# An eleventh weight slot, loaded between the two halves of the output projection's weights, and expert pairs written out

## The reference

```
mixed = sigmoid(gate_a) * (y_a @ moba_up) + sigmoid(gate_b) * (y_b @ hgrn_up)
x = x + mixed @ w_out
h2 = rmsnorm(x, norm2_w)
logits = h2 @ router_w + router_b            # top 4 of 32, softmax over the 4
gu = xg @ w_gate_up[e] + b_gate_up[e]        # 1024 -> 2048, for the tokens of expert e
y  = ((up + 1) * glu(gate)) @ w_down[e] + b_down[e]
out = rmsnorm(x + sum of w * y, final_norm_w)
```

## Time and profile before

| | us |
|---|---|
| median of three runs (1144.83 to 1147.44) | 1146.56 |
| the profiled execution's own time | 1146.84 |
| its span, first to last instruction | 1145.0 |
| TensorE busy | 1065.1 |
| VectorE busy | 349.5 |
| ScalarE busy | 222.9 |

### The profile page before, as it was taken

How to read it: one execution, slowest core, us unless ns; L and a number is a source line. 1 busy time by engine, 2 the same in 40 slices (tenths; PEclk the granted TensorE clock), 3 DMA queues, 4 the chain that set the end, 5 groups by cost and what they waited for, 6 DMA issues and landing times.

```text
span 1145.0 us, 13775 instructions
## 1 busy us (share of the span) xinstructions
PE 1065.1 (93%) x5611; PEld 521.7 (46%) x5611; DVE 349.5 (31%) x686; ACT 222.9 (19%) x354; POOL 37.5 (3%) x32
## 2 busy tenths in 40 slices
PE   7999999999999999998999898988888898999896
PEld 7789999734343443433333333333333333343332
DVE  4983788421213122121212111121212030213022
ACT  6734675301010101010101010100010101010002
POOL 0380000000000000000000000000000000000000
PEclk9999999999999999999999999999999998999999
DMA  9445658999999999999999999999999999999994
GB/s 324 163 159 185 265 187 291 367 369 430 428 428 428 430 428 427 428 428 430 425 428 429 428 428 426 430 428 429 430 425 430 428 429 425 428 430 428 428 428 191
DMA packets 46916, 439.28 MB, mean 384 GB/s; under 512 B 5324, under 2 KB 7656, under 8 KB 22152
## 3 DMA queue, kind: packets, MB, share of 16 engines
q1 hardware_dynamic: 44560, 436.78, 91.7%
q10 hardware_dynamic: 2296, 1.61, 0.5%
HBM read 437.32 MB, written 1.05 MB: 383 GB/s over the span
## 4 chain that ended last, share of the span: by engine, by line
PE 59%; DMA 36%; DVE 2%; issue 1%; SPq 1%; ACT 1%; DVEq 0%
PE PS L1652 23%; DMA S<-in_w_gate_up_dram 19%; PE PS L1702 11%; DMA EXTRA<-in_w_down_dram 8%; PE PS L1323 6%; DMA EXTRA<-in_w_gate_up_dram 4%; PE PS L1634 4%; DMA S<-in_w_down_dram 4%; PE PS L1614 3%; DMA S<-in_w_in_dram 1%; PE PS L1336 1%; PE PS L1339 1%; PE PS L1342 1%; PE PS L1689 1%; PE PS L1671 1%
## 5 line engine op out<-in xcount | busy, mean ns | idle before, releaser
L1652 PE MATMUL PS<-S,M 128*64 128x512 f32 x1664 | 378.7, 604 | 32.5 <-DMA S<-in_w_gate_up_dram 23.9
L1652 PEld LDWEIGHTS PS<-S,M 128*64 128x64 f32 x1664 | 115.9, 138 | 270.7 <-issue 222.7
L1702 PE MATMUL PS<-S,M 128*64 128x512 f32 x800 | 178.2, 595 | 18.2 <-DMA S<-in_w_down_dram 17.3
L1156 DVE TENSOR_SCALAR M<-PS 128x256 f32<-128x256 f32 x64 | 27.0, 422 | 537.2 <-PE PS L1652 537.2
L751 ACT ACTIVATE M<-M 128x256 f32<-128x256 f32 x64 | 26.7, 416 | 501.0 <-DVE M L1156 501.0
L1702 PEld LDWEIGHTS PS<-S,M 128*64 128x64 f32 x800 | 56.6, 137 | 129.0 <-issue 109.5
L756 ACT COPY M<-PS 64x512 f32<-64x512 f32 x31 | 17.9, 578 | 277.5 <-PE PS L1702 277.5
L1170 DVE COPY M<-PS 128x512 f32<-128x512 f32 x32 | 22.1, 692 | 131.1 <-PE PS L1689 131.1
L1614 PE MATMUL PS<-M,X 128*128 128x128 f32 x480 | 59.0, 281 | 0.0
L1614 PEld LDWEIGHTS PS<-M,X 128*128 128x128 f32 x480 | 57.7, 196 | 0.0
L1634 PE MATMUL PS<-M,SELT 128*128 128x512 f32 x120 | 55.5, 605 | 0.0
(11 more groups left out here) (255 smaller groups left out, 924.1 us busy)
## 6 DMA issues: line engine op xcount, KB each, us to landing
S<-in_w_gate_up_dram SPq DMA_DIRECT2D x104, 2048.0 KB, 43.0
S<-in_w_down_dram SPq DMA_DIRECT2D x49, 2048.0 KB, 42.1
M<-in_w_gate_up_dram SPq DMA_DIRECT2D x12, 2048.0 KB, 41.4
EXTRA<-in_w_gate_up_dram SPq DMA_DIRECT2D x12, 2048.0 KB, 42.4
S<-in_w_in_dram SPq DMA_DIRECT2D x10, 2048.0 KB, 8.1
EXTRA<-in_w_down_dram SPq DMA_DIRECT2D x7, 2048.0 KB, 43.4
M<-in_w_down_dram SPq DMA_DIRECT2D x7, 2048.0 KB, 42.0
S<-in_w_out_dram SPq DMA_DIRECT2D x2, 2048.0 KB, 8.3
```

Of the source, the lines that this page charges most:

```text
L1156: v.tensor_scalar(gate[:, c], g2[:, :, 0], LIMIT, None, ALU.min).then_inc(gate_ready, 1)
L1652: ins = mm(gu[half][64 * g:64 * g + 64, :], hTe[:, k, tok], gu_slot[slot][:, kk, c:c + 512], start=(k == 0), stop=(k == KD - 1))
L1702: ins = mm(multi[64 * n:64 * n + 64, :], actT[b][:, k, 64 * kh:64 * kh + 64], dn_slot[slot][:, k, 512 * n:512 * n + 512], start=(kh == 0 a ...
```

## The change

An eleventh slot B of 2 MB is added to the ring. Its memory is that of the former normalised rows XN, of one page of M and of front tables. The tables (attention mask, rotation tables, level masks) now lie inside B and are dead before the slot is filled; biases and router weights move to other pages. Squares and the final rows are written to other pages.

Since 60 is no multiple of 11, the pairs are written out on SyncE and TensorE. The load of FW moves from the end of the front to the point behind ScalarE's loop over the first 15 pairs, because its page is in use before. In the front two steps change places on TensorE and on VectorE. The constants are loaded in three transfers in place of two.

```diff
-SLOTS = 10
-CYCLE = 5
+SLOTS = 11
+PAIRS = E // 2
...
-        XN = sb("XN", [P, TT, D])
-        M = sb("M", [P, 13 * 1024])
+        B = sb("B", [P, 4096])
+        XN = B[:, 0:TT * D].rearrange("p (t d) -> p t d", t=TT)
+        M = sb("M", [P, 12 * 1024])
...
-        slots = [S[:, s, :] for s in range(8)] + [mpage(8, 4), EXTRA[:]]
+        slots = [S[:, s, :] for s in range(8)] + [mpage(8, 4), EXTRA[:], B[:]]
...
                 if what == "wo1":
+                    load(0, 0, 10)
                     sp.wait_ge(yb_ready, 1)
                     load(0, 0, 3)
...
-                    sp.dma_start(CST[:, 128:], A["cst"][:, 128:]).then_inc(cst_loaded, 16)
-                    sp.dma_start(MSK[:], A["lmask"].rearrange("p (m t) -> p m t", t=CHUNK)).then_inc(lmask_loaded, 16)
+                    sp.dma_start(CST[:, 128:512], A["cst"][:, 128:512]).then_inc(cst_loaded, 16)
+                    sp.dma_start(FRONT, A["cst"][:, 512:]).then_inc(cst_loaded, 16)
+                    sp.dma_start(MSK, A["lmask"].rearrange("p (m t) -> p m t", t=CHUNK)).then_inc(lmask_loaded, 16)
...
-            for m in (10, 11):
-                used(0, m - SLOTS)
-                load(0, 0, m)
-            with sp.Fori(0, 2) as c:
-                for j in range(1, CYCLE + 1):
-                    load_pair(c * CYCLE + j, c * (2 * CYCLE) + 2 * j, j)
+            used(0, 0)
+            load(0, 0, 11)
+            last = PAIRS - 1
+            for j in range(1, last):
+                load_pair(j, 2 * j, j)
...
-            wait_drained(se, "lg1")
-            se.dma_start(FW, A["final_norm_w"].unsqueeze(0).to_broadcast([P, D])).then_inc(fw_loaded, 16)
...
             with se.Fori(0, E // 2 - 1) as p:
                 pair(p)
+            se.dma_start(FW, A["final_norm_w"].unsqueeze(0).to_broadcast([P, D])).then_inc(fw_loaded, 16)
             pair(E // 2 - 1, last=True)
...
             residual(1, 1)
+            turned_in(1)
             first_places(0)
-            turned_in(1)
             chosen(1)
...
-                ins = mm(ps[:, 0:E], ucum, mask[:, tt, :], start=True, stop=(tt == 0))
-                if tt:
-                    ins = mm(ps[:, 0:E], ones, mask[:, 0, :], start=False, stop=True)
...
+            turned_x1(1, 1)
             places(0)
-            turned_x1(1, 1)
             for name in ("all", "wT"):
                 claim(name)
+            logits(1, 1)
             pe.wait_ge(first_sel_ready, 1)
             first_gather(0, 0)
-            logits(1, 1)
             first_gather(0, 1)
...
-            with pe.Fori(0, 2) as c:
-                for j in range(1, CYCLE + 1):
-                    pair(0, c, j)
-            pair(0, 2, 1)
-            pair(0, 2, 2, residual=True)
+            for j in range(PAIRS - 3):
+                pair(0, j, residual=(j == PAIRS - 4))
```

More of the change, by code:

```diff
@@ L137, in hybrid_block @@
             hT_hi = over("hT_hi", 2).rearrange("p (k t) -> p k t", k=KD)
+            over("skip_b2", 1, F32)
+            FRONT = early.enter_context(nc.sbuf_tensor("FRONT", [P, 512], F32))[:]
+            MSK = early.enter_context(nc.sbuf_tensor("MSK", [P, 512], I32))[:, 0:NMASK * CHUNK]
+            MSK = MSK.rearrange("p (m t) -> p m t", t=CHUNK)
             mix_hi = over("mix_hi", 2)
@@ L146, in hybrid_block @@
             hi_b = over("hi_b", 4)
-            over("skip_m12", 1, F32)
             over("skip_s0", 8, F32)
@@ L449, in load_pair @@
                     load(e, j, m)
-            for m in (10, 11):
-                used(0, m - SLOTS)
-                load(0, 0, m)
-            with sp.Fori(0, 2) as c:
-                for j in range(1, CYCLE + 1):
-                    load_pair(c * CYCLE + j, c * (2 * CYCLE) + 2 * j, j)
[L457 to L460, removed]
+            used(0, 0)
[3 more added lines that the diff above has]
+                load_pair(j, 2 * j, j)
+            load_pair(last, E - 2, last, stop=11)
             used(last, 11 - SLOTS)
-            last_slot = ring(CYCLE, 11)[0]
+            last_slot = ring(last, 11)[0]
             for part, done in ((0, slot_loaded[last_slot]), (1, last_loaded)):
@@ L473, in _ @@
                                 n = PER_ROUND[m] * SLOTS - SLOTS + m
-                                used(r * (E // 2) + (n // 12 - E // 2), n % 12)
+                                used(r * PAIRS + (n // 12 - PAIRS), n % 12)
                             else:
-                                used(r * (E // 2), m - SLOTS)
+                                used(r * PAIRS, m - SLOTS)
                             load(0, 0, m)
-                        with sp.Fori(0, 3) as c:
-                            for j in range(1, CYCLE + 1):
-                                load_pair(r * (E // 2) + c * CYCLE + j, c * (2 * CYCLE) + 2 * j, j)
+                        for j in range(1, PAIRS):
+                            load_pair(r * PAIRS + j, 2 * j, j)
             for n, (tt, half) in enumerate(((0, 0), (0, 1), (1, 0))):
@@ L1562, in places @@
                 ps = claim(f"pos{tt}")
+                if tt:
+                    mm(ps[:, 0:E], ones, mask[:, 0, :], start=True, stop=False)
                 pe.wait_ge(mask_ready, tt + 1)
-                ins = mm(ps[:, 0:E], ucum, mask[:, tt, :], start=True, stop=(tt == 0))
-                if tt:
-                    ins = mm(ps[:, 0:E], ones, mask[:, 0, :], start=False, stop=True)
-                end(ins, f"pos{tt}")
+                end(mm(ps[:, 0:E], ucum, mask[:, tt, :], start=(tt == 0), stop=True), f"pos{tt}")
             def hidden(tt, k):
@@ L1638, in arrived @@
             def arrived(at, m):
-                r, c, j = at
+                r, j = at
                 slot, before = ring(j, m)
-                pe.wait_ge(slot_loaded[slot], r * (16 * PER_ROUND[slot]) + c * 96 + (before * 16 + 16))
+                pe.wait_ge(slot_loaded[slot], r * (16 * PER_ROUND[slot]) + (before * 16 + 16))
                 return slot
@@ L1721, in add_residual, with pair @@
                            skip_group_check=True)
-            def pair(r, c, j, first=False, last=False, residual=False, final=False):
-                at, p = (r, c, j), r * (E // 2) + c * CYCLE + j
+            def pair(r, j, last=False, residual=False, final=False):
+                at, p, first = (r, j), r * PAIRS + j, j == 0
                 i = p * 2
@@ L1751, in last_pairs @@
             def last_pairs():
-                for j in range(3, CYCLE):
-                    pair(0, 2, j)
-                pair(0, 2, CYCLE, last=True, final=True)
+                for j in range(PAIRS - 3, PAIRS - 1):
+                    pair(0, j)
+                pair(0, PAIRS - 1, last=True, final=True)
                 pe.wait_ge(y_ready, E + 1)
                 pe.wait_ge(last_y_ready, 1)
-            pair(0, 0, 0, first=True)
-            with pe.Fori(0, 2) as c:
-                for j in range(1, CYCLE + 1):
-                    pair(0, c, j)
-            pair(0, 2, 1)
-            pair(0, 2, 2, residual=True)
+            for j in range(PAIRS - 3):
+                pair(0, j, residual=(j == PAIRS - 4))
             pe.wait_ge(rounds_ready, 1)
@@ L1770, in _ @@
                         pe.wait_ge(gu_drained, r * (2 * E) + 2)
[L1771 to L1777, removed]
+                        gather(r * PAIRS)
+                        for j in range(PAIRS):
+                            pair(r, j, last=(j == PAIRS - 1))
                         pe.wait_ge(y_ready, (r + 1) * E + 1)
@@ L1799, in shape_constants @@
     c[:, 128:256] = r[:, None] < r[None, :]
-    c[:, 256:384] = 1 + r[None, :] % CAP
+    c[:, 256:256 + CAP] = 1 + np.arange(CAP)[None, :]
+    for x in range(4):
+        c[E * x:E * x + E, 320 + E * (x % 2):320 + E * (x % 2) + E] = np.eye(E)
+    c[:, 384:512] = 1.0
     own = np.where(r[None, :] <= r[:, None], 0.0, NEG)
-    c[:, 384:512] = own
     c[:, 512:640] = own
+    c[:, 640:768] = own
     inv = (np.float32(10000.0) ** (-(np.arange(32, dtype=np.float32) * np.float32(2.0) / np.float32(DH)))).astype(np.float32)
@@ L1806, in shape_constants @@
     for t in range(TT):
[L1807 to L1811, removed]
+        c[:, 896 + 32 * t:928 + 32 * t] = np.cos(ang[P * t:P * t + P])
+        c[:, 960 + 32 * t:992 + 32 * t] = np.sin(ang[P * t:P * t + P])
     m = np.zeros((P, NMASK, CHUNK), np.int32)
```

52 lines of the change are left out of this document (27 added, 25 removed).

## The result

The changed kernel takes 1149.26 us (median of 8 runs, 1148.90 to 1149.94), the kernel before 1146.59 us (median of 8, 1144.83 to 1148.72). The ratio is 1.0029, 95% interval 1.0020 to 1.0037: slower by 2.7 to 3.3 us. The profiled execution took 1149.75 us, with a span of 1147.9 us, 2.9 us more than the span of before.

What follows compares the result with a forecast made beforehand. The bound was taken to be full transfers in the expert part, behind a front that leaves them idle. Slot -4.9, `wo1` +4.7, clock +1.6, FW +1.3 gave +2.7 us, 1149.3 us against the median; range 1142.8 to 1152.0.

Steps and rivals of the forecast that it cites:

- The other signs: In the changed trace: ScalarE's wait about 8.5 us, TensorE's stop about 5.4, first ring release about 236, landings 48.
- The slot, -4.9: In the expert part: the eleventh slot leaves one piece fewer behind the ring's first release, -4.9 us.
- `wo1` late by 5.4, TensorE by 4.7: In the front: B's load delays `wo1` by 5.4 us; less 0.72 us slack, TensorE starts 4.7 us later.
- The clock, 1.6: In the front: TensorE's longer stop is followed by a stretch at the lower clock, +1.6 us (0.8 to 2.4).
- FW, 1.3: Near 1079 us: FW's 0.52 MB enters the full queue and delays what is still to land, +1.3 us.
- Reorder, pairs written out, memory, 0 each: Front reorder 0 +- 0.3 us; written-out pairs 0, their 2.56 us stop being hidden; other pages, same instructions, 0.
- With `wo1` not late: Rival in the front: B doesn't hold up `wo1`, only slot and FW are left, -3.6 us, 1143.0; chance 0.2.
- Without the slow stretch: Rival in the front: `wo1` is late but the stop leaves no lower clock, +1.1 us, 1147.7; chance 0.15.

Runs made afterwards that it cites:

- Two experiments: Changed kernel with B's load moved behind `wo1`: 1142.96 us; changed kernel with the first half of `wo1` rounded behind the third piece of `mix_hi`: 1142.63 us.
- the fillers: Changed kernel with four filler matmuls on TensorE ahead of its wait for `mix_hi`, inside the stop: 1147.53 us, ratio 1.0008.
- FW last: FW's load on SyncE's queue behind the last piece: in the kernel before 1146.54 us; in the changed kernel with B loaded behind `wo1` 1143.08 us.
- the later rounding: Changed kernel, B's load left in place, ScalarE rounding the first half of `wo1` behind the third piece of `mix_hi`: 1142.63 us, ratio 0.9975.

## Why the prediction was right

The time was forecast at 1149.3 and measured at 1149.26. The mechanism was right, but so close a hit is luck: single terms were off by up to 0.9 us, and the errors nearly cancel. The other signs that the prediction named came too; landings took 48.1 us from issue in place of 43.0.

- **The slot, -4.9.** Right: -4.9 us by the medians and -5.6 by the ratios between ten and eleven slots with all else equal.
- **`wo1` late by 5.4, TensorE by 4.7.** Right in mechanism, a little large: 5.1 and 4.3 us. In the queue B landed at 181.5 us and the next piece 4.9 behind it, the lower end of what I allowed; the pair of transfers in the earlier trace rows had been too pessimistic. Two experiments undo the delay in two independent ways, and both return it whole.
- **The clock, 1.6.** The mechanism was right and the size was too small: 2.5 us. I had priced one slow stretch of 3.41 us, partly inside the stop. A stop of 5.0 us left 6.83 us at the lower level. My upper end, 2.4, was too low too.
- **FW, 1.3.** 1.0 to 1.2 us by the count of packets; the run times of FW late alone give 1.3 by the medians and 1.7 by the ratio, with an interval of 0.7 to 2.6.
- **Reorder, pairs written out, memory, 0 each.** Right for the front and the end: -0.1 us for the reorder between projection and first expert, and no gain with ten slots and the pairs written out. But the middle of the kernel is not quite the same. These are the packets from 300 to 1060 us in the kernel before and in the changed kernel with ten slots:

```profile
DMA packets 22335, 325.34 MB, mean 428 GB/s; under 512 B 2478, under 2 KB 2478, under 8 KB 2478
...
DMA packets 22316, 324.97 MB, mean 428 GB/s; under 512 B 2481, under 2 KB 2481, under 8 KB 2481
```

The four traces with loops move 325.34 to 325.39 MB in that stretch, the eight with the pairs written out 324.94 to 325.04. That is 0.8 us of transfer that the prediction had at nothing. Little of it reaches the end: to the last weight packet the count is 767.5 us with ten slots and the pairs written out, 767.1 with loops, both with FW late. Which part of the change slows the middle is not shown.

The sum with the measured terms is -4.9 + 4.3 + 2.5 + 1.1 = +3.0 us.

The rivals had the right prices too. With `wo1` not late I had worked out 1143.0, and that version took 1142.96. Without the slow stretch it was 1147.7, and the fillers gave 1147.53, though with a slow stretch elsewhere in the profiled execution. The Trainium skill (DMA: Bandwidth & Descriptors, Queues, rings and completion order) says that descriptors are consumed in ring order, though completion need not follow it. The trace is in line with the first half: B, the next piece and `wo1` landed in the order of their issue, at 181.5, 186.4 and 192.0 us. The Trainium skill (Runtime: NRT & Kernel Launch, Instruction fetch mechanics) says that a taken branch can stall the fetch of instructions. The stop of 2.56 us at the loop's turn is not in the trace of the changed kernel, and with ten slots and the pairs written out its absence brought no time.

What stays open: a version with B behind `wo1` and FW off the full stretch should be 4.9 us under the kernel before. With FW in the first pair the profiled span is 4.6 us shorter (1140.4 against 1145.0), but the run times are only 2.9 us lower by the ratio, 4.0 at the most by the interval; with FW last they are 3.6 us lower, and there the interval reaches 4.9. (By the medians it is 3.3 and 2.1 us.) The traces have most of the gain: from the start of the first expert to the landing of the last weight packet it takes 904.9 us in the kernel before, with the reorder alone and with FW last, and 900.5 and 899.8 us in the two versions. How often slow stretches fall into single executions may be why the run times show less; that was only argued, not tried.

Several versions beat both kernels: B behind `wo1` (0.9971), the later rounding (0.9975), B behind `wo1` with FW in the first pair (0.9975) and with FW last (0.9969). Among them no order can be told.

## What to carry to other kernels

When transfers bound the long part of a kernel and its front leaves them idle, memory for one more piece is worth about that piece's transfer time (4.9 us here), but only if its load holds up nobody: place it behind the last load that someone waits for, even if its memory is free earlier. Look for the waiter not at the engine that needs the data but at what stands behind the first touch of them in an in-order program; here three roundings that didn't need `wo1` carried the delay to TensorE. A small load belongs ahead of the last hole or behind the last piece; in between it cost about its own time here, 1.0 to 1.2 us, which the transfers show and the run times hardly do.

## What the runs showed of the hardware that I had not expected

A stop of TensorE of 4.99 us cost 2.5 us more than itself, through 6.83 us at a granted clock of 0.50. One of 1.49 us was not followed by a slow stretch.

Slow stretches also come where TensorE hardly stops, and not in every execution of the same code. In the first pair the kernel before has one, and the same code with only FW moved has none:

```profile
245.00:249.00 4.00, 4.00 (x15) 1.56 (x16) 1.02 (x2) 0.37 (x1) 0.00 (x0) 0.59 1.02 438
...
245.00:249.00 4.00, 4.00 (x23) 1.81 (x24) 0.75 (x2) 0.37 (x1) 0.00 (x0) 1.00 1.00 426
```

The first row is from the kernel before, the second from FW late alone. The fifth load came 21.5 us after the first in the one (251.54 - 230.03) and 19.9 us in the other (249.62 - 229.75). So chance moves an execution by 1.6 us there, as much as several of the terms that were to be measured. The runs of the kernel before spread from 1144.0 to 1148.7 us.
